# Second mixer's output product: how far ahead of TensorE its items are prepared

## The reference

```python
def short_conv_mixer(x, w_in, conv_w, w_out):
    proj = jnp.einsum('bsd,de->bse', x, w_in)
    gate_b, gate_c, h = jnp.split(proj, 3, axis=-1)
    z = gate_c * h
    zp = jnp.pad(z, ((0, 0), (CONV_WIDTH - 1, 0), (0, 0)))
    s = x.shape[1]
    conv = sum(conv_w[k] * zp[:, k:k + s] for k in range(CONV_WIDTH))
    return jnp.einsum('bse,ed->bsd', gate_b * conv, w_out)
```

## Time and profile before

| | us |
|---|---|
| median of three executions | 2071.82 (2071.81 to 2072.83) |
| the profiled execution | 2070.66 |
| its span, first to last instruction | 2068.9 |
| TensorE busy (matmul) | 2052.1 (99%) |
| VectorE busy | 1325.2 (64%) |
| ScalarE busy | 853.9 (41%) |
| GpSimd busy | 790.2 (38%) |

### The profile page before, as it was taken

The page is one execution under the profiler, slowest core; times in us unless marked ns, Lnnn a source line. Parts: engine busy times, 40 slices in busy tenths (PEclk is TensorE's granted clock), DMA queues, the critical chain, the costliest instruction groups (busy, mean ns, idle before and its releaser), DMA issues. The chain is left out here.

```text
span 2068.9 us, 25147 instructions
## 1 busy us (share of the span) xinstructions
PE 2052.1 (99%) x9437; PEld 1702.7 (82%) x9437; DVE 1325.2 (64%) x1677; ACT 853.9 (41%) x1241; POOL 790.2 (38%) x523
## 2 busy tenths in 40 slices
PE   9999999999999999999999999999999999999999
PEld 9888788888888888888878887888888888888887
DVE  4744775655666757564687769775655666666563
ACT  3112465454544334431433334655445543334430
POOL 5212157787702000212266751167877412000220
PEclk9999999999999999999999999999999999999999
DMA  5111123444589655411022238034444599554221
GB/s 189 42 62 45 38 82 137 144 161 156 197 309 390 218 201 182 141 34 41 21 88 86 87 133 299 1 122 145 150 158 142 205 382 362 185 202 153 97 87 41
DMA packets 190708, 306.05 MB, mean 148 GB/s; under 512 B 13472, under 2 KB 71932, under 8 KB 190588
## 3 DMA queue, kind: packets, MB, share of 16 engines
q1 hardware_dynamic: 189888, 304.14, 42.1%
q10 hardware_dynamic: 700, 0.31, 0.1%
HBM read 233.62 MB, written 70.78 MB: 147 GB/s over the span
## 5 line engine op out<-in xcount | busy, mean ns | idle before, releaser
L1326 POOL TENSOR_TENSOR w_lo<-raw,w_hi 128x512 fp32r<-128x512 f32 x92 | 131.0, 1455 | 744.0 <-ACT w_hi L1441 744.0
L1339 POOL TENSOR_TENSOR op_lo<-op_sum,op_hi 128x512 fp32r<-128x512 f32 x151 | 225.1, 1506 | 34.4 <-ACT op_hi L1643 28.5
L1608 ACT CAST hop_hi<-h_raw 128x1024 fp32r<-128x1024 f32 x124 | 130.4, 1051 | 257.0 <-PE bank_a L2367 155.4
L1643 ACT CAST op_hi<-op_sum 128x512 fp32r<-128x512 f32 x151 | 93.9, 622 | 329.5 <-POOL op_sum L1420 87.9
L2365 PE MATMUL bank_a<-wop_hi,hop_hi 128*128 128x512 f32 x576 | 224.2, 389 | 4.7 <-DVE resid L2153 4.7
L2131 DVE TENSOR_TENSOR hop_lo<-h_raw,hop_hi 128x1024 fp32r<-128x1024 f32 x124 | 152.0, 1226 | 117.5 <-ACT hop_hi L1608 117.3
L2367 PE MATMUL bank_a<-wop_hi,hop_lo 128*128 128x512 f32 x576 | 224.1, 389 | 0.0
L2366 PE MATMUL bank_a<-wop_lo,hop_hi 128*128 128x512 f32 x576 | 224.1, 389 | 0.0
L1339 POOL TENSOR_TENSOR op_lo<-w_raw,op_hi 128x512 fp32r<-128x512 f32 x115 | 164.2, 1428 | 116.4 <-ACT op_hi L1643 115.3
L2367 PE MATMUL bank_a<-xt_hi,op_lo 128*128 128x512 f32 x456 | 177.4, 389 | 0.0
L2365 PE MATMUL bank_a<-xt_hi,op_hi 128*128 128x512 f32 x456 | 177.4, 389 | 0.0
(11 more groups left out here) (243 smaller groups left out, 4879.4 us busy)
## 6 DMA issues: line engine op xcount, KB each, us to landing
w_raw<-in_ffn_w_dram SPq DMA_DIRECT2D x144, 512.0 KB, 6.8
h_raw<-h_spill SPq DMA_DIRECT2D x112, 512.0 KB, 5.2
h_spill<-h_tile SPq DMA_DIRECT2D x170, 256.0 KB, 2.1
w_raw<-in_ffn_w_dram SPq DMA_DIRECT2D x112, 256.0 KB, 3.3
w_raw<-in_od_w_in_dram SPq DMA_DIRECT2D x40, 256.0 KB, 3.3
w_raw<-in_od_w_out_dram SPq DMA_DIRECT2D x18, 512.0 KB, 7.6
raw<-in_ple_gate_w_dram SPq DMA_DIRECT2D x32, 256.0 KB, 3.5
h_spill<-h_tile2t SPq DMA_DIRECT2D x28, 256.0 KB, 2.0
```

The costliest lines, as they stand in the source:

```text
L1326: pool.tensor_tensor(lo, raw[:, n % NRAW, :], hi.bitcast(F32), ALU.subtract).then_inc(lo_split, 1)
L1339: pool.tensor_tensor(by_four(op_lo[s]), operand_raw(tr, b, op), by_four(op_hi[s]).bitcast(F32), ALU.subtract).then_inc(op_low, 1)
L1608: act.copy(hop_hi[k][:, :, :], h_raw[a.hop_chunk(i)][:, :, :]).then_inc(ahead_hi, 1)
L1643: act.copy(by_four(op_hi[s]), operand_raw(tr, b, op)).then_inc(op_high, 1)
```

## The change

The loop that appends the preparations gets a second condition. While i is below 8, item `nxt` is prepared only if it is at most two ahead of item i; from i = 8 on the condition is as it was.

```diff
         for i, (form, j) in enumerate(OD_ITEMS):
-            while nxt < len(OD_ITEMS) and (a.user_before(nxt) is None or a.user_before(nxt) < i):
+            while nxt < len(OD_ITEMS) and (i >= 8 or nxt <= i + 2) \
+                    and (a.user_before(nxt) is None or a.user_before(nxt) < i):
                 prepare(OD, nxt)
                 nxt += 1
             st = add("prod", item=i, layer=OD, head=form_heads.get(form))
```

## The result

The changed kernel takes 2076.7 us (median of 13 executions, 2075.21 to 2079.04) against 2071.67 for the kernel before (13, 2070.47 to 2072.83). The ratio is 1.0024 with a 95% interval of 1.0016 to 1.0032: slower, by about 5 us. The profiled execution took 2075.3, its span is 2073.6 against 2068.9.

The account below looks back on a forecast made before the run. TensorE, busy 99%, was taken to wait for VectorE's order, with VectorE almost without slack. Emptying m3 1.04 us earlier, other terms nothing, took the timed 2071.82 to 2070.8; range 2068.8 to 2073.8.

Parts of the forecast that it names:

- What bounds the stretch: Second mixer's output product: TensorE waits for VectorE's order of work; VectorE's own idle time falls from 4.0 to 3.0 us.
- The schedule up to m5: VectorE's old durations laid in the new order: item 4's wait gone, TensorE 4.55 us ahead at item 8.
- Four take 14.03: VectorE behind m5's emptying: preparations 10 to 13 at 3.51 us each, so m3 is emptied 1.04 us earlier.
- GpSimd's part of the slab follows, and nobody waits for it: GpSimd's work on the feed-forward slab comes after its loads; no engine needs it before the next layer.
- The moved preparation 10: VectorE owes one more preparation behind m5, so item 12 waits some 3.8 us instead of 0.34.
- Rival (b): Slab casts or a late slab delay item 10 through m7; costs 0 to 0.8, up to 1.5 us; 11%.
- Rival (c): The one long wait lowers TensorE's clock, so item 12 begins at half rate; 2070.8 to 2076.2 us; 22%.
- (a): All of the product's waits are saved, about 5.1 us, to 2066.7; needs VectorE slack after item 8; 4%.
- (d): The cap does nothing because preparations were held back by something else anyway; 2071.8 us; 3%.

Follow-up runs that it names:

- e1_slab_late: Changed kernel with the slab stage moved behind the normalisation after item 9 and GpSimd's gain-row scaling held until the last preparation is done; 2072.03 us.
- e5_cap6: Changed kernel with the cap lifted from item 6 on instead of item 8, slab stage left behind item 7; 2074.03 us, ratio 1.0012 to the kernel before.
- e6_cap6_slab_late: Changed kernel with the cap lifted from item 6 on and the slab stage moved behind the normalisation after item 9; 2066.47 us, ratio 0.9976.
- e8_warm_wide: Changed kernel with 30 matmuls of 128x512 on TensorE in the wait before item 12, into a bank nobody reads; 2073.59 us, ratio 1.0012.
- e4_warm: Changed kernel with 48 identity transposes on TensorE in the wait before item 12, into a bank nobody reads; 2074.84 us, ratio 1.0015.

## Why the prediction was wrong

Forecast 2070.8 with a range to 2073.8; measured 2076.7. The chance given to slower by over 0.2% was 5%.

**What bounds the stretch** was right. The two waits were VectorE's order, and VectorE had no slack: its wait at m5 fell from 4.0 to 3.0, as forecast.

**The schedule up to m5** was right to within 0.1 us: item 4 at 1259.96 (1259.91), m6 emptied at 1270.61 (1270.55), item 6 at 1271.44 (1271.37), m5's first bank at 1278.56 (1278.49).

**"Four take 14.03"** is the step that failed. I priced the preparations 10 to 13 by their pace in the trace of the kernel before, and two of them now stood beside GpSimd. They took 17.83, and 13.93 where GpSimd was out of the way (e1_slab_late). The sentence "GpSimd's part of the slab follows, and nobody waits for it" asked only who waits for its result, and not who shares the memory with it. The kernel before had shown the price: while GpSimd was making operands, VectorE's passes over SBUF took more than twice their time. Two of its rows that I had read past, the same line while GpSimd was at work and after it had stopped (at 1229.0):

```profile
1215.68 1.78 DVE L1836 SCALAR_TENSOR_TENSOR cv<-z,cols,cv 128x512 f32<-128x512 f32 x1
...
1230.85 0.74 DVE L1836 SCALAR_TENSOR_TENSOR cv<-z,cols,cv 128x512 f32<-128x512 f32 x1
```

The rule is in the Trainium skill, "SBUF — State Buffer", section "Who interferes with whom": a VectorE instruction with two inputs in SBUF contends with a GpSimd instruction that reads SBUF, not with one that only writes. The same section calls the pair of ports that the two engines share an exclusive lock. The runs agree: 2.3 to 2.9 instead of 1.22 beside subtractions and the scaling, 1.22 beside the writing of zeros (one overlap of 0.46), and 0.69 as ever for the emptying of m5, whose second input is in PSUM. The lock itself no run shows; the lengths fit it. It is the rule that I should have weighed against this change.

**The moved preparation 10.** I had the cost of this move in the sum (four preparations behind m5 in place of three) and had drawn the right result from it, a gain of only 1.04. e1_slab_late confirms the wait, 3.77 against 3.8 forecast. But I took the order of the queues as given and did not ask what the same cap would do if it ended two items earlier. Alone that takes 2.7 us off the changed kernel and is still slower than the kernel before (e5_cap6, 2074.03); with the slab late as well it is 5.2 faster than the kernel before (e6_cap6_slab_late).

**Rival (b)**, slab loads and casts in the way: not what happened. The slab's casts ended at 1283.4, preparation 10's cast at 1284.37, and VectorE began the pass that needs it at 1284.46, right behind its sum: there was 0.1 us to spare. Only in the profile of e8_warm_wide did it cost something, 0.54.

**Rival (c)**, the clock, came true, on top of the longer wait: 1.47 us in the profiled execution, within the bounds of 0 to 5.44, and its mechanism was the one described. The sum had put this term at nothing; a slow matmul costs 0.20 more (0.43 instead of 0.23), and in the other profiles with an unfilled wait item 12 lost 1.3 to 2.9 us. I gave it 22%. Alone it would have kept the time inside the range, as in e1_slab_late (2072.03). In all five profiles with an unfilled wait of 3.7 us or more before item 12 the clock fell; behind the wait of 3.0 it fell in two profiles and stayed up in one. That agrees with the page of the Trainium skill cited there, "TensorE: Matmul & The Clock Gate", Part 1, by which it matters where a gap falls. Taking the single 3.0 of the kernel before as a sign that 3.8 is more likely harmless than not was too hopeful. The two errors are of one make: a term was called free without a row of the old order that showed it to be so.

**Rivals (a) and (d)** fell: VectorE had no slack, and the cap did act.

## What to carry to other kernels

When a step is moved, list what every other engine runs in its new place, and look in the old trace for unusually long forms of the same instruction and what stood beside them: who shares memory access with whom counts as much as who waits for whom. A wait that is taken from the front of a chain comes back at its end unless the engine that sets the pace gets its idle time used: preparation 10 in VectorE's gap and GpSimd out of the way made 5.2 us faster what was 5.0 slower. A slow stretch of TensorE's clock cost nothing here ahead of another wait that was long enough to take it in (1.71 us), and its full price where no such wait followed. In this product a wait of 3.7 us or more brought one every time, waits of 3.0 in two of three, and unfilled waits up to 1.7 never, which speaks against gathering short waits into a long one.

## What the runs showed of the hardware

Passes of 128x1024 on VectorE with both inputs in SBUF took 2.3 us instead of 1.22 beside GpSimd's two-input passes of 128x512, and 2.9 where they met its scaling of 128x2048. GpSimd's four passes in turn took 7.0 instead of 5.05, and its scaling 2.77 instead of 1.91. Lengths of about two and two and a half passes fit engines that take turns, which no view shows directly.

Nearly the same order of work meets the clock in either state: the wait of 3.00 before item 4 left it at 1.00 in one profile and was followed by 0.50 in two. It also fell in e4_warm, where 48 transposes of 128 columns filled most of the wait and only 2.2 us stood empty, and it did not fall in e8_warm_wide, where full-width matmuls filled it to within 0.5.
